# Feed-forward's up product in seven half products instead of eight, over two groups of 640 tokens

## The reference, cut to what matters

```python
xp = xp + g1 * merge(o_gla, gg, gla_norm[l], o_swa, w_o[l])
h = adaln(xp, norm_ff[l], sh2, sc2)              # [1280 tokens, 1024]
xp = xp + g2 * sq_relu_mlp(h, w_ff1[l], w_ff2[l])

def sq_relu_mlp(h, w1, w2):                      # w1 [1024, 4096], w2 [4096, 1024]
    return jnp.square(jax.nn.relu(h @ w1)) @ w2
```

## Time and profile before

| | us |
|---|---|
| median of 3 runs (lowest, highest) | 1818.78 (1816.28, 1823.18) |
| the profiled execution's own time | 1818.8 |
| its span, first to last instruction | 1816.7 |
| start of the transposes behind the last projection tile | 917.6 |
| last adding of the hardware loop on DVE | 1747.3 |
| last DVE instruction of the feed-forward | 1812.4 |

### The profile page before, as it was taken

How to read it: one execution, slowest core, us unless ns; L and a number is a source line. 1 busy time by engine, 2 the same in 40 slices (tenths; PEclk the granted TensorE clock), 3 DMA queues, 4 the chain that set the end, 5 groups by cost and what they waited for, 6 DMA issues and landing times.

```text
span 1816.7 us, 24375 instructions
## 1 busy us (share of the span) xinstructions
PE 1721.0 (95%) x9082; PEld 1383.0 (76%) x9082; DVE 850.4 (47%) x1343; ACT 468.9 (26%) x734; POOL 619.1 (34%) x450
## 2 busy tenths in 40 slices
PE   4999999987999988989999999999999999999997
PEld 1898788876656653458878888888888888888885
DVE  2624656647566677525543332223332223332278
ACT  2413223313333434422231112211112211112210
POOL 1611545624341466402253323323223323223320
PEclk9999999997899999999999999999999999999999
DMA  8254565657343434423331101111111011111024
GB/s 315 78 146 134 182 223 173 226 163 196 128 148 114 147 110 138 139 87 120 125 104 47 47 23 46 35 35 46 37 32 46 27 43 46 34 35 46 23 81 173
DMA packets 167461, 186.08 MB, mean 102 GB/s; under 512 B 51552, under 2 KB 132576, under 8 KB 164320
## 3 DMA queue, kind: packets, MB, share of 16 engines
q1 hardware_dynamic: 165296, 185.14, 32.0%
q10 hardware_dynamic: 2096, 0.02, 0.1%
HBM read 140.52 MB, written 44.61 MB: 102 GB/s over the span
## 4 chain that ended last, share of the span: by engine, by line
PE 52%; DVE 2%; issue 1%; DMA 1%; POOL 0%; ACT 0%; DVEq 0%; ACTq 0%
PE ff_banks L2364 8%; PE ff_banks L2365 8%; PE ff_banks L2366 8%; PE ff_banks L2337 7%; PE ff_banks L2339 7%; PE ff_banks L2338 7%; PE ff_banks L2047 2%; PE ff_banks L2045 2%; PE ff_banks L2046 2%; DVE ff_acc L2260 1%; PE ff_banks L2033 1%; DMA mid_raw<-x 1%; PE ff_banks L2055 0%; DVE ff_acc L2265 0%; DVE mrg_h L2024 0%
## 5 line engine op out<-in xcount | busy, mean ns | idle before, releaser
L2257 DVE TENSOR_TENSOR ff_acc<-ff_acc,ff_banks 128x512 f32<-128x512 f32 x280 | 192.6, 688 | 187.6 <-PE ff_banks L2366 187.6
L2338 PE MATMUL ff_banks<-h_lo,h_whi 128*128 128x512 f32 x744 | 263.3, 354 | 0.0
L2337 PE MATMUL ff_banks<-h_hi,h_whi 128*128 128x512 f32 x744 | 263.2, 354 | 0.0
L2339 PE MATMUL ff_banks<-h_hi,h_whi 128*128 128x512 f32 x744 | 263.1, 354 | 0.0
L2364 PE MATMUL ff_banks<-h_whi,h_wlo 128*128 128x512 f32 x640 | 250.0, 391 | 3.8 <-POOL h_wlo L2217 2.5
L2365 PE MATMUL ff_banks<-h_whi,h_wlo 128*128 128x512 f32 x640 | 249.8, 390 | 0.0
L2366 PE MATMUL ff_banks<-h_whi,h_wlo 128*128 128x512 f32 x640 | 249.7, 390 | 0.0
L2211 POOL TENSOR_TENSOR h_whi<-mid_raw,h_whi 128x1024 fp32r<-128x1024 f32 x32 | 77.7, 2453 | 317.7 <-ACT h_whi L2162 317.7
L2337 PEld LDWEIGHTS ff_banks<-h_hi,h_whi 128*128 128x128 f32 x744 | 140.6, 189 | 20.1
L2338 PEld LDWEIGHTS ff_banks<-h_lo,h_whi 128*128 128x128 f32 x744 | 140.6, 189 | 20.0
L2339 PEld LDWEIGHTS ff_banks<-h_hi,h_whi 128*128 128x128 f32 x744 | 140.6, 189 | 19.5
(11 more groups left out here) (231 smaller groups left out, 3159.2 us busy)
## 6 DMA issues: line engine op xcount, KB each, us to landing
mid_raw<-in_w_ff SPq DMA_DIRECT2D x64, 512.0 KB, 3.9
mid_raw<-in_w_ada SPq DMA_DIRECT2D x18, 1024.0 KB, 7.1
gla_qk<-qk_by_channel SPq DMA_DIRECT2D x20, 512.0 KB, 4.1
proj<-prj_stage SPq DMA_DIRECT2D x60, 152.0 KB, 1.9
mid_raw<-in_w_in SPq DMA_DIRECT2D x6, 1216.0 KB, 6.5
head_slices<-in_w_ada SPq DMA_DIRECT2D x6, 1024.0 KB, 11.0
decays<-prj_run SPq DMA_DIRECT2D x8, 640.0 KB, 4.3
gla_bc<-decays SPq DMA_DIRECT2D x20, 256.0 KB, 2.8
```

The lines of the kernel that those rows point to most:

```text
L2257: dve.tensor_tensor(acc[:, p, at], acc[:, p, at], down[n % RING], ALU.add).then_inc(added, 1)
L2337: pe.matmul(out, w_hi[:, k, :], hi[:, k, t0:t1], start=(k == 0), stop=False)
L2338: pe.matmul(out, w_hi[:, k, :], lo[:, k, t0:t1], start=False, stop=False)
L2339: mm = pe.matmul(out, w_lo[:, k, :], hi[:, k, t0:t1], start=False, stop=(k == KD - 1))
```

## The change

The up product of each group of 640 tokens is done with one level of Strassen's scheme (in Winograd's form). Tokens are halved (320 and 320), input channels are halved (512 and 512), and two blocks of hidden channels, q and q + 16 of the group's 16 pairs, form the halves of the weight. Seven products of 4 x 128 channels by 320 tokens take the place of eight. For that:

- The tokens are done in two groups, A (tiles 0 to 4) and B (tiles 5 to 9). Each group goes through all 16 pairs, so both weights are loaded and split twice. `acc` holds one group.
- `Operands` makes the seven combinations of h for a group once: four sums or differences on DVE, seven roundings on ACT and seven low parts (four on POOL, three on DVE), each of 128 x 1280 elements. For A this is done in the last merge tiles, for B during the last two down products of A. h of B goes through memory and comes back as `hb`.
- Per pair DVE makes four sums of weight halves (`weights_sum`, 128 x 512 each), ACT seven roundings and POOL seven low parts of 128 x 512 (`high1`, `low1`).
- Per pair the seven products use three banks (order 0, 1, 2, 0, 1, 2, 1). One is copied out by ACT (`copy`) and seven additions on DVE (`evict`, 128 x 320, bank plus SBUF) combine them into four hidden parts. ACT then does Relu and Square twice (once rounded, once not) for each part (`hidden`).
- The down products of pair q come after the up products of pair q + 1. A group's last two down products stand together, and so do the first two up products.
- At A's end `acc` is scaled, gets the residual and is stored while B's first two up products run.

```diff
+                for i in range(3):
+                    product(0, i)
                 mrg.pe_norm(pe, NT - 1)
+                for i in range(3, 7):
+                    product(0, i)
+                group(0)
+                x.done(pe, 1)
+                up(PAIRS)
+                group(1)
...
+                def product(q, i):
+                    first = isinstance(q, int) and q == 0
+                    pe.wait_ge(w1lo_ready, 7 * q + i + 1)
+                    if first and i == 2:
+                        pe.wait_ge(mrg.gated, NT - 1)
+                    if not first and i < 3:
+                        pe.wait_ge(evicted, 7 * q - (4, 0, 1)[i])
+                    if i == 3:
+                        pe.wait_ge(copied, q + 1)
+                    if i > 3:
+                        pe.wait_ge(evicted, 7 * q + (1, 2, 5)[i - 4])
+                    w_hi, w_lo = weight(q, i)
+                    x_hi, x_lo = x.high(i), x.low(i)
+                    out = bank[(0, 1, 2, 0, 1, 2, 1)[i]]
+                    for k in range(KH):
+                        pe.matmul(out, w_hi[:, k], x_hi[:, k], start=(k == 0), stop=False)
+                        pe.matmul(out, w_hi[:, k], x_lo[:, k], start=False, stop=False)
+                        mm = pe.matmul(out, w_lo[:, k], x_hi[:, k], start=False, stop=(k == KH - 1))
+                    mm.then_inc(up_ready, 1)
...
+                def group(g):
+                    q0 = PAIRS * g
+                    up(q0 + 1)
+                    down_products(q0, 0, False)
+                    with pe.Fori(q0 // 2 + 1, q0 // 2 + PAIRS // 2 - 1) as i:
+                        up(2 * i)
+                        down_products(2 * i - 1, 1, False)
+                        up(2 * i + 1)
+                        down_products(2 * i, 0, False)
+                    q = q0 + PAIRS - 2
+                    up(q)
+                    down_products(q - 1, 1, False)
+                    up(q + 1)
+                    down_products(q, 0, False)
+                    down_products(q + 1, 1, True)
...
+                def step(q, j):                    # ScalarE
+                    high2(q - 1, 0)
+                    copy(q)
+                    high2(q - 1, 1)
+                    for i in range(4):
+                        hidden(q, j, i)
+                    for i in range(7):
+                        high1(q + 1, i)
...
+                def weights1(q, g):                # SyncE
+                    sp.wait_ge(w1lo_ready, 7 if isinstance(q, int) and q == 2 else 7 * q)
+                    for m in range(2):
+                        load1(q, g, m)
```

814 lines of the change are left out of this document (557 added, 257 removed).

## The result

| us | before | changed |
|---|---|---|
| median (lowest, highest), 15 runs each | 1823.18 (1816.28, 1828.50) | 1813.52 (1807.02, 1816.57) |
| ratio of the runs, 95% interval | | 0.9943 (0.9929 to 0.9958) |
| span of the profiled execution | 1816.7 | 1811.8 |

The change saves 9.7 us, 0.6%. 1794 was forecast, from 1778 to 1809: the result lies 4.5 us above the range, and the saving, forecast as 24.4 us, is 0.4 of that. A later set of 8 runs (e11) gave 0.9948 (0.993 to 0.9966).

What follows compares the result with a forecast made beforehand. PE's own work was taken to bound the feed-forward. 1818.8 - 46.1 (up products) + 1.9 (A's start) + 22.2 (A to B) - 2.4 (tail) = 1794.4, so 1794 us, range 1778 to 1809.

Steps and rivals of the forecast that it cites:

- -46.1 us: Up products, whole feed-forward: 24.64 us instead of 27.52 for both groups, 2.88 us saved 16 times.
- The steady step is costed at nothing: Steady loop: DVE, ACT and POOL all keep up with PE's 25.9 us per pair, so no loss.
- that rival: Wait in every step: DVE's readings of bank 1 delay the seventh product 32 times, 1828 or 1833 us; chance 0.07.
- +1.9 us: A's start: late copies, a late weight and half clock lose 9 us against 7.1 before; bounds 0 and +8.
- Sum 9: A's start: total us lost to the copies of pairs 0 and 1, pair 1's second weight and half clock.
- +22.2 us: From A to B: PE's waits plus half clock behind them; bounds 5 and 32.
- 10.5 + 4.3 + 1.5 + 2.5: From A to B, PE's waits: B's start, its second up product's weights, pair 17's copy, the seventh product.
- After the 2.7 us wait at 932 ... Twice: 3.4 us: From A to B: half clock after waits costs 1.7 us as in the earlier trace, counted twice.
- w1 for pair 17 comes late behind two gates and three residual tiles: From A to B: a late load in one queue, named as part of the seams longer rival.
- -2.4 us: Tail: 9 to 9.5 us lost where 11.4 were; bounds -6 and +3.
- then they take turns: Before B: DVE and POOL alternate on the operands, so PE waits 10.5 us; without exclusion 2.8.
- seams longer: Rival: late hand-overs move the next ones, +10 between A and B and +6 at the start, 1810 us; chance 0.13.

Runs made afterwards that it cites:

- e11: The changed kernel again, unedited, 8 runs: 1813.34 us, 0.9948 of before.
- e4: Changed kernel with the last of the seven products made twice, 12 more matmuls per pair and group: 1864.6 us.
- e5: Changed kernel with ACT's copies of pairs 0, 1 and 17 after the fifth rounding of the neighbouring pair's weights instead of the seventh: 1804.4 us.
- e3: Changed kernel with the load of w1 for pair 18 behind A's first store instead of behind all five: 1809.7 us.
- e12: Changed kernel with POOL's low parts of w2 for the last two pairs cut to one column, result incomplete: 1804.8 us.
- e6: Changed kernel with B's operands made one pair earlier, same instructions in other places: 1805.6 us.
- e7: Changed kernel with e3, e5 and e6 together, and the roundings of pair 17's weights between the hidden values of pair 16: 1800.9 us.
- e9: e7 with ACT's and POOL's halves of w2 for pair 15 ahead of B's last operands: 1793.3 us.
- e10: e9 with A's scalings and residual additions one by one among pair 16's evictions, only four left in pair 17's: 1795.19 us, 0.9839 of before.
- e13: e10 with POOL's low parts of four of B's operands cut to one of 128 columns, result incomplete: 1788.2 us.
- e14: e10 with POOL's four low parts of B's operands made by DVE, nothing left out: 1792.20 us, 0.9832 of before.

## Why the prediction was wrong

1813.5 measured, 1794 forecast: 19 us. 4.4 of them are the base: I worked from a profile at 1818.8 and a median of three that equals it, the median of fifteen is 1823.2. From that base my range would have ended at 1813.4, so the time would have missed it by a hair; the saving, 9.7 us for 24.4, would be as far off as it is. Together with 2.4, 9.1 and 1.3 us of the terms below and 0.9 of the merge tiles that makes 18.1; the last us lies between the lengths of two single traces and the medians. Term by term:

- **"-46.1 us", the up products: right.** 0.1466 us at 320 columns where I took 0.1467; e4 confirms it from the other side.
- **"The steady step is costed at nothing": right.** PE is busy 250 of 250 us. In the loop bank 1 never held it up, so that rival is out (at the seams it did: 3.5 us in pair 17 and 3.3 in pair 31, behind DVE's scalings). The DVE rows at 320 elements take 0.49 us as taken, those of ACT 0.47; POOL's 128 x 512 from `tmp` take 1.69 on average instead of 1.30, which the slack took.
- **"+1.9 us" at A's start: 4.3.** I had the copy of pair 0 late by 1.2 us; it was 2.24, since it stood behind two roundings that wait for the fourth sum of weights. There are two half-clock stretches (935.2 to 938.6 and 948.9 to 952.3), where I had counted one. My "Sum 9" was also not what I listed: 1.2, 2.2, 2.5 and 1.7 make 7.6. e5 takes away what the two copies and their half clock cost.
- **"+22.2 us" from A to B: 31.3. This is the step that failed**, and within it one term. The waits came near by luck: 10.5 + 4.3 + 1.5 + 2.5 = 18.8 forecast, 20.1 measured. Before B they are 6.6 us, not 10.5, and PE never waits for the copy of pair 17 itself; one of 3.8 us that I hadn't listed fills the gap. "After the 2.7 us wait at 932 ... Twice: 3.4 us" was wrong by a factor of three. Four stretches at half clock follow the waits, 20.7 us of PE's work, and cost 10. I counted two waits, and gave each the length of the stretch in the earlier trace rows, 3.4 us; here PE works 3.4, 3.4, 5.8 and 8.1 us in them. So of the 9.1 us that the seam is longer than forecast, 7 are this term, 1.3 are waits, and some 1 has no name.
- The one wait that I had not on the list is that of 3.83 us in the down product of pair 16, for w1 of pair 18. I had written of a queue in which "w1 for pair 17 comes late behind two gates and three residual tiles", as a rival; one pair later the same queue was late by 8 us. e3 shows it. The lesson is in my own list: I followed the queue to pair 17 and stopped.
- **"-2.4 us" for the tail: -1.1.** 49.8 forecast as 49; by my own figures 49 - 39.5 - 11.4 is -1.9, and the sum used -2.4. The mechanism (DVE beside POOL) was right; e12 measures it at 5.7 us.
- **The exclusion of DVE and POOL: right, and stronger than I used it.** I applied it to a chain ("then they take turns") and so believed that an earlier chain would be a free one. e6, e7 and e9 show that it is the sum of work that counts: in e10 the five longest of DVE's seven operand instructions there (the expectation of e13 says eight) take 9.3 us more than the 1.49 of each alone. The Trainium skill (SBUF — State Buffer, section "Who interferes with whom") says that the two exclude each other for a whole instruction where DVE has two SBUF inputs and GpSimd's instruction reads SBUF. This case agrees: 3.49 us for 1.49 (e10), 3.43 for 1.22 (tail), while DVE's additions with one input in a bank stay at 0.68 beside a busy POOL.

Of the rivals, *seams longer* is what happened, at 1813 instead of its 1810. I gave it 0.13. The measured 0.57% lies just on the side of 0.5% that had 0.87, and its interval, 0.42 to 0.71%, spans that line.

Two things stay open. e10's pairs 16 and 17 still take 33.8 us for 24.6, and e14's 35.3; which of POOL's weights and DVE's evictions would have to go was not tried, nor was leaving one or two of the low parts with POOL, which is idle for 15 us in e14. And the start's 2.5 us wait for POOL was left alone.

## What to carry to other kernels

Price a seam in two parts, the waits and the stretch at half clock behind each, and take for the second more than the shortest one seen. Where two engines exclude each other, add up both engines' time on such work over the whole window before moving anything: where the sum was too large here, four orders gave 1.4 us and a shorter or cheaper instruction 6, and giving work to the faster of the two shortened the window by 5.6. Then look at what the relieved engine does next: here it was late with the weights behind the window. Follow every in-order queue past the seam until its late entries have caught up, not only to the next load.
